# First weight sum of the quarter-block pairs: VectorE's add replaced by an accumulating transfer on GpSimd's queue

## The reference, cut to what matters

```
def swiglu(x, w_gate, w_up, w_down):
    return (jax.nn.silu(x @ w_gate) * (x @ w_up)) @ w_down

x = x + swiglu(rmsnorm(x, norm_ffn), ffn_w_gate, ffn_w_up, ffn_w_down)
```

## Time and profile before

| | us |
|---|---|
| median of three runs | 1376.54 |
| profiled execution | 1377.11 |
| its span, first to last instruction | 1375.3 |
| TensorE busy | 1362.6 |
| VectorE busy | 945.8 |
| ScalarE busy | 605.6 |
| GpSimd busy | 121.2 |

### The profile page before, as it was taken

How to read it: one execution, slowest core, us unless ns; L and a number is a source line. 1 busy time by engine, 2 the same in 40 slices (tenths; PEclk the granted TensorE clock), 3 DMA queues, 4 the chain that set the end, 5 groups by cost and what they waited for, 6 DMA issues and landing times.

```text
span 1375.3 us, 18326 instructions
## 1 busy us (share of the span) xinstructions
PE 1362.6 (99%) x6952; PEld 1135.4 (83%) x6952; DVE 945.8 (69%) x1296; ACT 605.6 (44%) x837; POOL 121.2 (9%) x142
## 2 busy tenths in 40 slices
PE   9999999999999999999999999999999999999997
PEld 7777777888788888888888788888888899989986
DVE  7757788555666765764676786777878689548944
ACT  6545677343444533432334544442244445325532
POOL 1010157000000000000000321015000000000000
PEclk9999999999999999999999999999999999999999
DMA  7232245422112333222331322332222342332321
GB/s 269 83 108 77 99 148 187 160 97 79 62 61 92 103 116 119 92 92 92 99 112 65 112 103 92 107 124 75 91 94 92 97 147 94 109 106 93 101 83 62
DMA packets 28031, 144.14 MB, mean 105 GB/s; under 512 B 3146, under 2 KB 8547, under 8 KB 13368
## 3 DMA queue, kind: packets, MB, share of 16 engines
q1 hardware_dynamic: 24616, 133.71, 28.2%
q0 software_dynamic: 2656, 8.72, 1.8%
q10 hardware_dynamic: 688, 0.73, 0.2%
HBM read 136.84 MB, written 6.30 MB: 104 GB/s over the span
## 4 chain that ended last, share of the span: by engine, by line
PE 94%; DVE 2%; ACT 1%; DMA 1%; issue 1%; SPq 0%; POOL 0%; DVEq 0%; ACTq 0%
PE ps L2091 28%; PE ps L2093 28%; PE ps L2092 28%; PE ps L2513 1%; PE ps L2315 1%; PE ps L2328 1%; PE ps L2463 1%; PE ps L2305 1%; DMA f_out<-f_out_dram 1%; PE ps L2354 1%; PE ps L2649 1%; PE ps L2651 1%; PE ps L2655 1%; PE ps L2356 0%; PE ps L2355 0%
## 5 line engine op out<-in xcount | busy, mean ns | idle before, releaser
L2091 PE MATMUL ps<-opA_hi,w_hi 128*128 128x512 f32 (+1 forms) x1008 | 387.4, 384 | 0.9 <-DVE w_lo L1270 0.4
L2093 PE MATMUL ps<-opA_hi,w_lo 128*128 128x512 f32 (+1 forms) x1008 | 380.9, 378 | 0.0
L2092 PE MATMUL ps<-opA_lo,w_hi 128*128 128x512 f32 (+1 forms) x1008 | 380.5, 377 | 0.0
L700 ACT CAST w_hi<-raw 128x2048 fp32r<-128x2048 f32 x111 | 212.0, 1910 | 248.8 <-PE ps L2093 248.5
L1270 DVE TENSOR_TENSOR w_lo<-raw,w_hi 128x2048 fp32r<-128x2048 f32 x112 | 256.7, 2292 | 90.1 <-ACT w_hi L700 88.7
L2091 PE MATMUL ps<-opB_hi,w_hi 128*128 128x512 f32 (+1 forms) x584 | 226.7, 388 | 1.7 <-DVE opB_lo L1306 1.0
L2092 PE MATMUL ps<-opB_lo,w_hi 128*128 128x512 f32 (+1 forms) x584 | 225.7, 386 | 0.0
L2093 PE MATMUL ps<-opB_hi,w_lo 128*128 128x512 f32 (+1 forms) x584 | 225.6, 386 | 0.0
L2091 PEld LDWEIGHTS ps<-opA_hi,w_hi 128*128 128x128 f32 x1008 | 189.8, 188 | 38.4 <-issue 2.9
L2092 PEld LDWEIGHTS ps<-opA_lo,w_hi 128*128 128x128 f32 x1008 | 189.8, 188 | 35.5 <-issue 1.7
L2093 PEld LDWEIGHTS ps<-opA_hi,w_lo 128*128 128x128 f32 x1008 | 189.7, 188 | 35.6
(11 more groups left out here) (444 smaller groups left out, 2009.5 us busy)
## 6 DMA issues: line engine op xcount, KB each, us to landing
raw<-weights_dram SPq DMA_DIRECT2D x113, 1024.0 KB, 4.9
g_dram<-g_stage POOLq DMA_DIRECT2D x8, 512.0 KB, 3.0
h<-x_t_dram SPq DMA_DIRECT2D x7, 512.0 KB, 6.3
g_spec<-g_dram SPq DMA_DIRECT2D x5, 512.0 KB, 3.4
scores<-g_dram SPq DMA_DIRECT2D x3, 512.0 KB, 5.0
out_dram<-h SPq DMA_DIRECT2D x6, 256.0 KB, 2.3
mem_raw<-mem_t_dram POOLq DMA_DIRECT2D x1, 1024.0 KB, 8.9
c_keys<-c_dram POOLq DMA_DIRECT2D x4, 256.0 KB, 3.7
```

What stands on the lines that cost most here:

```text
L700: A.copy(w_hi[:, p, :], raw[:, p, :]).then_inc(hi_ready, 1)
L2091: W.matmul(out, w[0], x[0], start=start, stop=False, skip_group_check=mixed)
L2092: W.matmul(out, w[0], x[1], start=False, stop=False, skip_group_check=mixed)
L2093: return W.matmul(out, w[1], x[0], start=False, stop=stop, skip_group_check=mixed)
```

## The change

The add s1 leaves VectorE. In its place GpSimd issues, for each of the 14 quarter pairs, a transfer that reads quarter (1, 1) of the pair's weights from DRAM once more (128 rows of 2 KB) and adds it to quarter (1, 0) in `raw`. It is issued when the pair's raw load has landed and when `s_hi` of the quarter pair before has been made (for k = 0 only the former). It counts up `mid_in`, under the name `s1_added`, by 16. ScalarE (`pair_hi`) and VectorE (`sums`) wait for that count in place of VectorE's.

```diff
-        m_done, m_copied, s1_made, s_made, c12_made, s_hi_made, s_lo_made = st_done, st_hi, late_half, inv_read, st_lo, pn_done, skipped
+        m_done, m_copied, s1_added, s_made, c12_made, s_hi_made, s_lo_made = st_done, st_hi, mid_in, inv_read, st_lo, pn_done, skipped
+        S1_BASE = 32
...
+            for g, k in W_COUNT.items():
+
+                pool.wait_ge(raw_in[g % 2], 16 * (g // 2))
+                if k:
+                    pool.wait_ge(s_hi_made, BY_8 + k)
+                pool.dma_start(quarter(raw, g % 2, 1, 0), a["weights"][in_dram(g)][:, CHUNK + T:2 * CHUNK], accum_op=ALU.add
+                               ).then_inc(s1_added, 16)
...
             def pair_hi(g):
                 if g in W_COUNT:
-                    act.wait_ge(s1_made, BY_8 + W_COUNT[g] + 1)
+                    act.wait_ge(s1_added, S1_BASE + 16 * (W_COUNT[g] + 1))
...
-            def s1(g):
-
-                if g in W_COUNT:
-                    p = g % 2
-                    dve.wait_ge(raw_in[p], 16 * (g // 2))
-                    V.tensor_tensor(quarter(raw, p, 1, 0), quarter(raw, p, 1, 0), quarter(raw, p, 1, 1), ALU.add).then_inc(s1_made, 1)
-
             def sums(g):
                 if g in W_COUNT:
                     p, k = g % 2, W_COUNT[g]
-                    dve.wait_ge(s1_made, BY_8 + k + 1)
+                    dve.wait_ge(s1_added, S1_BASE + 16 * (k + 1))
...
-                s1(g + 3)
```

## The result

The change made the kernel slower: 1392.97 us (median of four runs, 1391.51 to 1393.44) against 1376.51 us, a ratio of 1.0118 (95% interval 1.0106 to 1.0130), 16.5 us. The forecast was 1376.6.

What follows compares the result with a forecast made beforehand. TensorE was taken to bound the kernel. 1377.11 us for the profiled execution, less 0 for the removed adds, plus 0 for the transfers, set against the 1376.54 median, gave 1376.6 us; range 1375.8 to 1387.

Steps and rivals of the forecast that it cites:

- What bounds the kernel: Second feed-forward block: TensorE, busy 99% of the span, runs its quarter pairs at one rate, with nothing to gain.
- the price of the removed adds: Fourteen VectorE adds, 0.684 us each, 9.6 us of busy time, lie off TensorE's path: gain 0.
- Part 2 (a): Steady quarter pairs: each transfer links s_hi of one pair to the next pair's sums; free up to 6.5 us, cost 0.
- G: Time from the end of s_hi of one quarter pair to the next pair's sums; forecast 4.2 us, between 3.2 and 7.9.
- Part 2 (b): Opening of the first long group: two transfers in line before TensorE wants m1's bank; cost 2G - 9.83, nothing up to G = 4.9.
- Part 2 (c): Landing time of each accumulating transfer on GpSimd's queue: 4.0 us, low end 2.9, high end 7.7.
- the tri case: Earlier 256 KB transfer issued 1.0 us before a 1 MB load, landed after 3.0 us; taken as the model for the new transfers.
- the mask case: Earlier 256 KB transfer issued 0.6 us after a 1 MB load, landed after 5.2 us.
- The raw loads: Raw loads sharing the engines with transfers may land up to 1.3 us later; cost 0, costing only from 4 us on.
- The rule on a blocked descriptor write: GpSimd's transfer descriptors cannot be written while VectorE is in a 2-port mode; judged not to apply to tensor_tensor.
- rival three: VectorE's w_lo delays GpSimd's descriptors by up to 2.29 us: 3.2 us in the opening, 1379.7 us; chance 0.03.
- Rival one: Late transfers stall sums and w_hi of the quarter pairs: 1378.7 to 1394.8 us; chance 0.14 below 0.2%, 0.23 above.

Runs made afterwards that it cites:

- e8_nos1: The kernel before with the first weight sum left out, no add on VectorE and no transfer: 1376.53 us against 1376.42, ratio 0.9999.
- e13_steady: Changed kernel, but quarter pairs 0 and 1 get their sum from VectorE as before; transfers 2 to 13 still released by s_hi: 1384.55 us, ratio 1.0064.
- e5_opening: Changed kernel with only transfer 1 released early, by transfer 0's landing instead of s_hi of pair 0: 1388.88 us, ratio 1.0089 to the kernel before.
- e1_early: Changed kernel with each transfer released by its own raw load and the transfer before it, not s_hi: 1378.53 us against 1376.42 for the kernel before.
- e2_plain: Changed kernel with plain transfers of the same 256 KB, without the addition, same queue and waits: 1378.85 us, ratio 1.0017 to the kernel before.
- e11_half: Changed kernel with transfers of half the size, 128 rows of 1 KB: 1386.04 us (two runs), ratio 1.0070 to the kernel before.

## Why the prediction was wrong, point by point

- **What bounds the kernel; the price of the removed adds.** Right. TensorE had no slack to give; e8_nos1 has the adds gone and the time unchanged.
- **Part 2 (a), the threshold G = 6.5 and the loop of G + 3.55.** Right. At G = 7.4 the loop turns in 10.94 us, and four late links a group give 3.7 to 3.9 us (e13_steady). Four, not five, in group one too: link 2 has more room. In the kernel before, s_hi of pair 1 ends at 1118.83 and the sums of pair 2 start at 1126.14, so 7.3 us lie between them, and I had taken 6.5 for every link. In e5_opening, whose opening runs late, the fifth link is late as well.
- **Part 2 (b), the opening.** The chain is right: with the raw load down at 1102.16 and gaps of 7.99 and 7.30 us it puts the m1 copy's end at 1102.16 + 7.99 + 3.55 + 7.30 + 3.55 + 0.27 = 1124.82, and TensorE's product starts at 1124.84. Two things were missing. Pair 0's w_lo is late as well (TensorE begins the pair 0.5 us late in the kernel after, 0.84 in e1_early), and the long wait drops the clock (2.2 us). Of the 8.5 us that the timed runs give the opening, the traces show 10.75 - 3.86 = 6.9 inside group one and those 0.5 us before it; the last 1.1 us are laid to no cause here.
- **Part 2 (c), the landing: this is the step that failed.** The prediction took 4.0 us, "the tri case", because the transfer would be 0.7 us ahead of the raw load; it landed after 6.9. The size of the transfer itself was right: alone it takes 4.1 to 4.2 us. The overlap with the load was wrong, and in two steps. First, the head start was 0.32 us and not 0.7, since GpSimd issues 0.54 us after the end of s_hi, where I had put 0.1. Second, and this counts for more, 0.7 us would not have been enough. Transfer 0 got the head start that was forecast for it (0.65 us) and landed after 7.7 us, and no accumulating transfer of this size that was less than 1.2 us ahead landed in under 6.5 us. The tri row was 1.0 us ahead and plain; the accumulating transfer's packets start later, 1.57 us after the issue against 1.24, and its issue row is longer by the same 0.3 us (0.86 against 0.54). Two cases 1.6 us of issue time apart stood in the earlier trace rows and nothing between them, and I put the edge on the favourable side. With 5.2 us, the mask case, the prediction's own formula gives 1.0 us, in the opening alone; the rest is the add behind a load, 6.9 in place of 5.2 (e2_plain).
- **The raw loads.** The one beside transfer 0 took 7.2 us in place of 4.9, a steady one (1148.54) 5.5. In the steady pairs this cost nothing, as worked out: in the kernel after each landed 4 to 6 us before the transfer that also waits for it was issued.
- **The rule on a blocked descriptor write; rival three.** No sign: GpSimd's issue lasts 0.85 to 0.87 us in all but the first two (0.94 and 0.88), alone or beside VectorE's w_lo. The Trainium skill, SBUF — State Buffer, section "Who interferes with whom", says that tensor_tensor has no 2-port mode and did not stall a DMA in its probe; the trace agrees.
- **Rival one came true.** Its price formula gave 18.3 us at G = 7.9 and 8.4 at 7.0; at 7.4 it gives 5.0 + 5 x 0.9 + (4 x 0.9 - 0.3) = 12.8 and, with 2.2 for the clock, 15.0, against 16.5 measured. The prediction had no term for the clock and none for pair 0's w_lo. I gave this rival 0.23 and ended the range at G = 7.2, though my own bounds for G reached to 7.9.

What stays open: why the transfer's packets wait for most of the load once the load's have started, why the first transfer is 1 us slower than the others, and the 1.1 us of the opening. Head starts between 0.65 and 1.2 us were not tried.

## What to carry to other kernels

A transfer that is issued at about the same time as a big load is not priced by its own size: price it as if it landed after the load, unless its issue stands well ahead (here 1.2 us gave 4.9 us, 1.6 us gave 4.1). Compare when the first packets of the two start, and not only when they are issued. Moving work off an engine that isn't the bound buys nothing, but the new wait can close a loop (here s_hi, transfer, sums, s_hi) whose length must be compared with the period of the bounding engine. Release such a transfer by the earliest condition that keeps it safe, which here was its own data and the transfer before it.

## What the runs showed of the hardware

- An accumulating transfer of 256 KB from DRAM, issued by GpSimd, lands after 4.1 us alone and 6.9 us when a 1 MB load is issued 0.3 us behind it; a plain one after 3.3 and 5.2 us. Its issue holds GpSimd's queue for 0.86 us against 0.54.
- The first packet starts 1.57 us after the issue of an accumulating transfer on GpSimd's queue, 1.24 us after that of a plain one there, and 0.96 us after that of a 1 MB load on SyncE's queue, each with the engines free. When the load was issued 0.3 us or less behind it (kernel after, e13_steady), the accumulating transfer's first packet started 4.2 to 4.7 us after its issue.
- GpSimd issues 0.54 us after the end of the ScalarE instruction that it waits for (in the kernel after 0.57 once and 0.85 once).
- TensorE's granted clock fell to 0.50 in waits of 4.4, 3.7 and 2.8 us (kernel after, e11_half, e5_opening), and stayed there for 5.2, 3.0 and 6.0 us of full work behind them; in waits of up to 1.4 us it did not fall.
